# Feed-forward down projection: from eight block products per block pair to seven, on one Trainium2 core

## The reference, cut to what matters

```
x = x + merged @ w_o
h = _rms_norm(x, g_ffn)
u = jnp.square(jax.nn.relu(jnp.einsum('bld,df->blf', h, w_up)))    # D_MODEL = 2048 -> D_FF = 8192
return x + jnp.einsum('blf,fd->bld', u, w_down)                    # 8192 -> 2048
```

## Time and profile before

| | us |
|---|---|
| median of three runs | 3292.89 (3292.1 to 3293.08) |
| the profiled execution: span | 3293.0 |
| PE busy in it | 3158.8 (96%) |
| DVE busy | 1949.6 (59%) |
| ACT busy | 1439.7 (44%) |
| up projection, from its first loads to its last matmul | about 1885 to 2528 |
| down projection with the output | 2528 to 3293 |

### The profile page before, as it was taken

The page is one execution under the profiler, slowest core; times in us unless marked ns, Lnnn a source line. Parts: engine busy times, 40 slices in busy tenths (PEclk is TensorE's granted clock), DMA queues, the critical chain, the costliest instruction groups (busy, mean ns, idle before and its releaser), DMA issues.

```text
span 3293.0 us, 66551 instructions
## 1 busy us (share of the span) xinstructions
PE 3158.8 (96%) x24759; PEld 3020.4 (92%) x24759; DVE 1949.6 (59%) x2700; ACT 1439.7 (44%) x1998; POOL 342.2 (10%) x623
## 2 busy tenths in 40 slices
PE   6999999999999999899889699999999999999999
PEld 6999999999999998775389699999999999999999
DVE  4225666665555558899843687887876333433333
ACT  4224666665555556677722344444443122121211
POOL 1111111111111113233300000000000000000000
PEclk9999999999999999999999899999999999999999
DMA  6434333333343338799953244444445323333322
GB/s 186 114 107 110 102 97 99 106 101 93 108 114 93 106 96 297 270 362 326 377 188 102 90 129 128 128 132 135 135 134 191 128 93 115 115 117 122 120 90 91
DMA packets 506127, 472.92 MB, mean 144 GB/s; under 512 B 19680, under 2 KB 435312, under 8 KB 504856
## 3 DMA queue, kind: packets, MB, share of 16 engines
q1 hardware_dynamic: 465616, 353.80, 36.1%
q0 software_dynamic: 40416, 117.93, 10.4%
HBM read 426.85 MB, written 44.80 MB: 143 GB/s over the span
## 4 chain that ended last, share of the span: by engine, by line
PE 88%; DVE 6%; DMA 3%; ACT 1%; issue 1%; POOL 0%; SPq 0%; POOLq 0%; ACTq 0%; DVEq 0%
PE ps L901 26%; PE ps L902 26%; PE ps L903 26%; PE ps L1084 3%; PE ps L1095 2%; PE ps L1096 2%; PE ps L1017 2%; DMA pg<-in_cache_fox_v_dram 1%; DVE pg_lo L1773 1%; PE ps L1127 1%; PE ps L1126 1%; PE ps L948 1%; DMA x2T<-xT_dram 0%; DVE qp_lo L1773 0%; DVE w_lo L1773 0%
## 5 line engine op out<-in xcount | busy, mean ns | idle before, releaser
L901 PE MATMUL ps<-h_hi,w_hi 128*128 128x260 f32 (+1 forms) x2592 | 750.0, 289 | 16.1 <-DVE h_lo L1773 13.0
L902 PE MATMUL ps<-h_hi,w_lo 128*128 128x260 f32 (+1 forms) x2592 | 737.3, 284 | 0.0
L903 PE MATMUL ps<-h_lo,w_hi 128*128 128x260 f32 (+1 forms) x2592 | 736.5, 284 | 0.0
L1773 DVE TENSOR_TENSOR w_lo<-w_raw,w_hi 128x2048 fp32r<-128x2048 f32 (+1 forms) x241 | 466.8, 1937 | 275.4 <-ACT w_hi L1323 239.6
L1323 ACT ACTIVATE w_hi<-w_raw 128x2048 fp32r<-128x2048 f32 x160 | 305.9, 1912 | 693.0 <-PE ps L903 680.1
L901 PE MATMUL ps<-ub_hi,w_hi 128*128 128x260 f32 x2048 | 581.6, 284 | 9.9 <-DVE xd L2184 5.5
L903 PE MATMUL ps<-ub_lo,w_hi 128*128 128x260 f32 x2048 | 580.4, 283 | 0.0
L902 PE MATMUL ps<-ub_hi,w_lo 128*128 128x260 f32 x2048 | 580.2, 283 | 0.0
L901 PE MATMUL ps<-b_hi,w_hi 128*128 128x260 f32 x1792 | 508.3, 284 | 29.6 <-DVE b_lo L1773 25.2
L901 PEld LDWEIGHTS ps<-h_hi,w_hi 128*128 128x128 f32 x2592 | 491.4, 190 | 19.6 <-DVE h_lo L1773 14.5
L902 PE MATMUL ps<-b_hi,w_lo 128*128 128x260 f32 x1792 | 508.3, 284 | 0.0
(11 more groups left out here) (303 smaller groups left out, 5160.4 us busy)
## 6 DMA issues: line engine op xcount, KB each, us to landing
w_raw<-in_w_in_dram SPq DMA_DIRECT2D x81, 1024.0 KB, 5.7
w_raw<-in_w_down_dram SPq DMA_DIRECT2D x64, 1024.0 KB, 5.4
w_raw<-in_w_up_dram SPq DMA_DIRECT2D x32, 1024.0 KB, 8.3
x2T<-in_w_up_dram SPq DMA_DIRECT2D x64, 512.0 KB, 5.4
pg<-in_cache_sb_v_dram POOLq DMA_DIRECT2D x106, 256.0 KB, 4.9
w_raw<-in_cache_fox_k_dram SPq DMA_DIRECT2D x72, 256.0 KB, 5.4
u_dram<-x2T SPq DMA_DIRECT2D x64, 260.0 KB, 3.0
u_st<-u_dram SPq DMA_DIRECT2D x8, 2080.0 KB, 7.8
```

Of the source, the lines that this page charges most:

```text
L901: pe.matmul(out, whi, xhi, start=first, stop=False, skip_group_check=more)
L902: pe.matmul(out, wlo, xhi, start=False, stop=False, skip_group_check=more)
L903: return pe.matmul(out, whi, xlo, start=False, stop=last, skip_group_check=more)
L1773: return dve.tensor_tensor(out, a, hi.bitcast(F32), ALU.subtract)
```

## The change: what it does, and the diff

The down projection gets the form of the up projection. The 8192 hidden features are taken in 4 chunks of 2048 (two halves, even and odd blocks, of 8 blocks each); in a chunk there are 8 pairs of output blocks, and each pair is a 2x2 block product of seven products (`down`, the same `product`, `high`, `low` and `weight_sum` as in the up projection). There are 4 x 8 x 7 = 224 products of 24 matmuls.

The seven token operands of a chunk (u11, t6, u21, t5, u12, t7, t4: blocks of u and differences of them) are formed in the up projection: DVE gets four more subtractions of 128 x 260 for a pair (t5, t6, t7 in the place of u12, t4), and POOL stores seven such blocks a pair (`store`) where SP stored four. At the start of each chunk the seven operands for the whole chunk (128 x 2080 each, 1.065 MB) are loaded one after the other into `b_lo`'s slot (`block_load`), each as soon as the last pair of the chunk before has finished the product that used this slot. For slots 0, 2, 4 and 6 ACT then makes the high part and DVE the low part in place. For slots 1, 3 and 5 (`NEG`) ACT makes the high part and then writes its negative into the low part's place, and a transfer issued by POOL adds the operand from DRAM to it (`block_add`, two transfers of half the block each with `accum_op`). There is one set of slots, not two.

The results go straight from the accumulation banks to `xd` by seven additions of DVE, the first 780 wide, the others 260 wide. The weights are loaded in four quarters of 0.5 MB a pair, in both projections, from a single list (`weights`); one of the quarters (`a22`) has two buffers, the others have one, and each is reloaded as soon as the low part that read it last is made. Their runs in DRAM are 512 bytes long (1024 bytes before in the down projection). The order of loads, ACT and DVE in the up projection changes a little: low part 4 comes before the first weight sum, low part 5 comes after the second. The turned result goes back into `xd` in place of `yn`, for each pair two quarter-megabyte stores.

```diff
-S_WO, S_FF = 81, 97
-FC = 1024
-NC = FF // FC
+S_WO = 81
 NU = FF // (2 * P)
-KF = FC // P
+KF = 8
+NC = NU // KF
...
+NEG = (1, 3, 5)
...
-        u_dram = nc.dram_tensor("u_dram", [FF // P, P, TQ], F32).ap()
+        u_dram = nc.dram_tensor("u_dram", [7, P, NU, HQ], F32).ap()
...
+        b_raw = b_lo[:, :, :, :].bitcast(F32)
+        xd = at("xd", [P, KT, TQ], F32, at_r)
+        u7 = [x2T[:, 8:15, HQ * i:HQ * i + HQ] for i in range(2)]
+        u_p1, u_p16, u_p165 = (x2T[:, k, 0:HQ] for k in (7, 6, 5))
...
+        a11, a12, a21 = w_raw[0][:, 0:8, :], w_raw[0][:, 8:16, :], w_raw[1][:, 0:8, :]
+        a22 = [w_raw[1][:, 8:16, :], a22_odd[:, :, :]]
...
+            def weights(g, b11, b12, b21, b22):
+                wait(sp, a_lo, count(g, 7, -7))
+                sp.dma_start(a22[g.p], b22).then_inc(a22_ld[g.p], 16)
+                wait(sp, a_lo, count(g, 7, -5))
+                sp.dma_start(a11, b11).then_inc(a11_ld, 16)
+                wait(sp, a_lo, count(g, 7, -2))
+                sp.dma_start(a21, b21).then_inc(a21_ld, 16)
+                wait(sp, a_lo, count(g, 7, -1))
+                sp.dma_start(a12, b12).then_inc(a12_ld, 16)
...
+            def store(g):
+                pool.wait_ge(r_ok, count(g, 2, 2))
+                pool.wait_ge(u_ok, count(g, 3, 3))
+                pool.wait_ge(t_ok, count(g, 4, 4))
+                dst = u_dram[:, :, g.n:g.n + 1, :] if not g.mult else u_dram[:, :, bass.ds(g.x * 2 + g.n, 1), :]
+                pool.dma_start(dst.rearrange("s p o t -> p s (o t)"), u7[g.p]).then_inc(u_sv[g.p], 16)
...
+            def block_load(g, c, i):
+                pool.wait_ge(p_ok, count(g, 7, i + 1))
+                pool.dma_start(b_raw[:, i, :, :], u_dram[i, :, c * KF:c * KF + KF, :]).then_inc(blk_ld[i], 16)
+            def block_add(g, c, i):
+                pool.wait_ge(blk_neg, count(g, 3, NEG0 + NEG.index(i) + 1))
+                for k in (0, 4):
+                    pool.dma_start(b_raw[:, i, k:k + 4, :], u_dram[i, :, c * KF + k:c * KF + k + 4, :],
+                                   accum_op=ALU.add).then_inc(blk_ld[i], 16)
...
+            for i in range(7):
+                block_load(Pair(NU - 1), 0, i)
+                if i == 0:
+                    store(Pair(NU - 2))
+                if i == 4:
+                    block_add(Pair(0), 0, 1)
+            for i in (3, 5):
+                block_add(Pair(0), 0, i)
+            store(Pair(NU - 1))
+            pool.wait_ge(x2_sw, 16)
+            for p in range(2):
+                pool.wait_ge(u_sv[p], 8 * NU)
+            pool.dma_start(xd[:, 4:KT, :], x2_dram[:, 4:KT, :]).then_inc(xd_ld[1], 16)
...
+            for c in range(1, NC):
+                for i in range(7):
+                    block_load(Pair(NU + KF * c - 1), c, i)
+                    if i == 4:
+                        block_add(Pair(c), c, 1)
+                for i in (3, 5):
+                    block_add(Pair(c), c, i)
...
+                if fresh is not None:
+                    i = AT[o]
+                    if i in NEG:
+                        pe.wait_ge(blk_ld[i], count(fresh, 48, 64))
+                    else:
+                        pe.wait_ge(blk_lo, count(fresh, 4, i // 2 + BLK0 + 1))
...
-            def down(c, par, u, j, first=False, between=None):
...
-                                        k == 0, k == KF - 1)
-                        mm.then_inc(dense_ok, 1)
...
+            def down(g, fresh=None, turned=None):
+                a, b, c = g.p, 2 + g.p, 4 + g.p
+                if g.q == 1:
+                    pe.wait_ge(r_ok, 2 * NU)
+                    pe.wait_ge(c_ev, 5 * NU)
+                pe.wait_ge(e_ok, count(g, 7, -14 + 3))
+                product(g, 1, a, True, False, fresh)
+                pe.wait_ge(e_ok, count(g, 7, -14 + 6))
+                product(g, 6, b, True, False, fresh)
+                pe.wait_ge(e_ok, count(g, 7, 1))
+                product(g, 2, a, False, False, fresh)
+                if turned is not None:
+                    turn(turned)
+                pe.wait_ge(e_ok, count(g, 7, 2))
+                product(g, 5, b, False, False, fresh)
+                pe.wait_ge(e_ok, count(g, 7, -14 + 7))
+                product(g, 7, c, True, False, fresh)
+                if turned is not None:
+                    turn_samples(turned)
+                pe.wait_ge(e_ok, count(g, 7, 4))
+                product(g, 3, b, False, False, fresh)
+                pe.wait_ge(e_ok, count(g, 7, 5))
+                product(g, 4, c, False, False, fresh)
...
+            def block_high(c, i):
+                act.wait_ge(blk_ld[i], count(c, 48 if i in NEG else 16, 32))
+                act.activation(b_hi[:, i, :, :], b_raw[:, i, :, :], ACT.Copy).then_inc(blk_hi, 1)
+                if i in NEG:
+                    act.wait_ge(blk_hi, count(c, 7, i + BLK0 + 1))
+                    act.activation(b_lo[:, i, :, :], b_hi[:, i, :, :].bitcast(F32), ACT.Copy, scale=-1.0).then_inc(blk_neg, 1)
...
+            def down(g, nxt, old=None, new=None, done=None):
+                high(g, 7)
+                if old is not None:
+                    block_high(old, 4)
+                high(g, 3)
+                if old is not None:
+                    block_high(old, 5)
+                if new is not None:
+                    block_high(new, 0)
+                high(g, 4)
+                if old is not None:
+                    block_high(old, 6)
+                if new is not None:
+                    block_high(new, 1)
+                if done is not None:
+                    turned(done)
                 if nxt is not None:
+                    high(nxt, 5)
+                    high(nxt, 1)
+                if new is not None:
+                    block_high(new, 2)
+                if done is not None:
+                    turned_samples(done)
+                if nxt is not None:
+                    high(nxt, 6)
+                if new is not None:
+                    block_high(new, 3)
+                if nxt is not None:
+                    high(nxt, 2)
...
+            def block_low(c, i):
+                if i in NEG:
+                    return
+                dve.wait_ge(blk_hi, count(c, 7, i + BLK0 + 1))
+                minus(b_lo[:, i, :, :], b_raw[:, i, :, :], b_hi[:, i, :, :]).then_inc(blk_lo, 1)
...
+                low(g, 4)
+                weight_sum(nxt, 1)
                 dve.wait_ge(p_ok, count(g, 7, 4))
+                dve.tensor_tensor(u_p165, u_p1, b, ALU.add).then_inc(c_ev, 1)
+                if new is not None:
+                    block_low(new, 0)
+                weight_sum(nxt, 2)
+                low(nxt, 5)
                 dve.wait_ge(p_ok, count(g, 7, 5))
                 dve.wait_ge(c_ev, count(g, 5, 2))
+                wait(dve, u_sv[g.p], count2(g, 16, 0))
+                dve.tensor_tensor(u22, u_p165, c, ALU.add).then_inc(c_ev, 1)
+                low(nxt, 1)
+                relu_square(u22, 3)
+                if new is not None:
+                    block_low(new, 1)
+                weight_sum(nxt, 3)
+                dve.wait_ge(p_ok, count(g, 7, 6))
+                dve.tensor_tensor(u12, u_p1, b, ALU.add).then_inc(c_ev, 1)
+                low(nxt, 6)
+                relu_square(u12, 4)
+                dve.wait_ge(r_ok, count(g, 2, 2))
+                dve.wait_ge(u_ok, count(g, 3, 2))
+                dve.tensor_tensor(t5, u12, u11, ALU.subtract).then_inc(t_ok, 1)
+                if new is not None:
+                    block_low(new, 2)
+                dve.wait_ge(p_ok, count(g, 7, 7))
+                dve.tensor_tensor(u21, u_p16, c, ALU.add).then_inc(c_ev, 1)
+                dve.wait_ge(t_ok, count(g, 4, 1))
+                dve.tensor_tensor(t6, u22, t5, ALU.subtract).then_inc(t_ok, 1)
+                dve.tensor_tensor(u12, u22, u12, ALU.subtract).then_inc(t_ok, 1)
+                low(nxt, 2)
+                relu_square(u21, 5)
+                weight_sum(nxt, 4)
+                dve.wait_ge(u_ok, count(g, 3, 3))
+                dve.wait_ge(t_ok, count(g, 4, 2))
+                dve.tensor_tensor(t4, u21, t6, ALU.subtract).then_inc(t_ok, 1)
+                if new is not None:
+                    block_low(new, 3)
...
+            def down(g, nxt, old=None, new=None):
+                m = 2 * g.q
+                a, b, c = (ps[:, r + g.p, 0:HQ] for r in (0, 2, 4))
+                x11, x12, x21, x22 = (xd[:, m + i, h * HQ:(h + 1) * HQ] for i in range(2) for h in range(2))
+                x3 = xd[:, m:m + 2, :].rearrange("p m t -> p (m t)")[:, HQ:4 * HQ].rearrange("p (o t) -> p o t", o=3)
+                def add(n, x, bank, before=None):
+                    dve.wait_ge(p_ok, count(g, 7, n))
+                    if before is not None:
+                        dve.wait_ge(e_ok, count(g, 7, before))
+                    dve.tensor_tensor(x, x, bank, ALU.add).then_inc(e_ok, 1)
+                if g.q in (0, 2):
```

(47 more changed lines are left out.)

514 lines of the change are left out of this document (198 added, 316 removed).

## The result

The changed kernel takes 3341.48 us (median of 4 runs, 3337.87 to 3344.11) against 3292.98 for the kernel before: 1.5% slower, ratio 1.0146 with a 95% interval of 1.0131 to 1.016. The forecast was 3228, range 3194 to 3265: wrong in sign, and outside the range by 76 us. The profiled execution has a span of 3340.0 us.

A forecast was written before the change was run, and what follows sets the result against it. The prediction took PE's number of matmuls as the bound. A floor of 3184.7 us, + 31.6 for boundaries, + 2.2 store, + 4 clock, - 2.7 up projection's start, + 8 a21 loop, gave 3227.8; range 3194 to 3265.

The forecast's parts named there:

- The removed work: Down projection: 5376 matmuls in place of 6144, 768 fewer at 0.1197 us, 91.9 us saved.
- change-over wait of the old kind: Between up and down projection: 16.3 us of waits and slow clock, expected to go.
- half shared, the load takes about 4.9: Up projection: a21's load overlapping POOL's store takes 4.9 us, period 20.3 to 20.4, +8 us in all, ends 0 and 25.
- The loop: Up projection: a21's single-buffer load, first weight sum, DVE's work (15.4 us) and low part 7 follow one another each pair.
- the lone load: Up projection: a 512 KB quarter by itself lands in 3.9 us, for a period of 19.4 us, hidden.
- 31.6 + 2.2 + 4: Chunk boundaries: block transfers 7.9 us late at each of four, first boundary's store +2.2, slow clock after waits +4.
- slot 5 then follows in time: Chunk boundary: after lateness at slots 1 and 3, together 7.9 us, slot 5 adds none.
- runs beside the transfers' lateness: Chunk boundary: DVE's overrun, 1 to 2 us for each of two pairs, overlaps late transfers and adds nothing.
- the adding transfer: Chunk boundary: an add costs the same as a plain transfer of its size; upper end twice that, 5.1 us for 1.065 MB.
- The clock: Chunk boundaries: lower clock after PE's waits costs 1 us each, +4, from 0.8 us behind one earlier gap.
- The loop in full force: Rival, chance 0.18: a21's loop makes up pairs 20.9 us, 17 us over the forecast, 3245.
- The slower rival: Chance 0.06: adding transfers at boundaries are a slow kind; 9.0 us each to pass 3299.6, 3312 at 10 us.

The follow-up runs named there:

- run 2: The changed kernel with low part 7 of the next pair moved on DVE ahead of the fourth weight sum and the last subtraction: 3269.26 us, ratio 0.9926.
- run 6: The changed kernel with POOL's store of pair n held until the first weight sum for pair n + 2 is made: 3270.17 us, ratio 0.9935.
- run 8: run 2's kernel with DVE's additions 4 and 5 before the first weight sum ahead of a chunk, weights 2 ahead of blocks 3 and 2: 3256.48 us.
- run 7: run 2's kernel with PE's loop over the first three chunks of the down projection written out: 3256.9 us, ratio 0.9888.
- run 3: The changed kernel without the adding transfers, so its results are wrong (a probe of time alone): 3329.66 us.
- run 10: run 9's kernel without the adding transfers, the low parts in slots 1, 3 and 5 staying negative high parts: 3244.09 us.
- run 9: The changed kernel with the three edits of run 2, run 7 and run 8 together: 3260.71 us, ratio 0.9905.
- run 12: run 11's kernel with block loads 1 to 6 held back until a21 and a12 land, and DVE's block 3 low part moved later: 3269.07 us.
- run 11: run 9's kernel with DVE making all seven low parts, without negative copies or adding transfers: 3250.36 us, ratio 0.9868.

## Why the prediction was wrong

Point by point, by its own steps.

**The removed work was right.** 5376 matmuls, 20.1 us a down pair, and no change-over wait of the old kind. The sum of the parts reproduces the span within 1 us. (The start of the up projection was forecast 2.7 us shorter and came 6.0 shorter.)

**The up projection: right mechanism, wrong size, by 62 us.** The step that failed is "half shared, the load takes about 4.9". The loop was named with the right links and nearly the right length on DVE (15.4 predicted, 15.3 measured); the lone load was right (3.9 predicted, 3.9 measured in runs 2 and 6). The load beside the store took 7.35 us up to the sum in the pair shown and lands after 7.0 in the median. I had sized the collision as a fair share of two streams over their overlap, 1.0 us. It cost 3.1. And I had bounded the load from above by the 5.4 us of a group of four, a row in which a transfer competes only with its own queue; no row showed two queues meeting in full, so this was not a bound. A period of 15.4 plus a load L is a slope of 1 us a pair, 30 us in all, for each microsecond of L above 4.7: so sensitive a term should have carried a wide end of its own.

**The boundary: 92.5 us for a predicted 31.6 + 2.2 + 4.** The step that failed is its model: I asked when the blocks land, and took everything else as hidden beside it. PE's list above shows what was late at the second boundary: first DVE's fourth addition (2.56), because a weight quarter took 9.2 us to land and DVE keeps its order; then PE's own instructions after the jump (4.29 and 2.12); only then a block transfer (5.54), the third add. The runs give sizes to these, with the others in place: order on DVE 3 us a boundary in the mean (run 8), the jump 6 at each of the two boundaries that have one (run 7), the adds 3 to 4 (runs 3 and 10). They can't be summed, since behind each wait stands the next (run 9). Two sentences of the prediction were plainly wrong: "slot 5 then follows in time", and that DVE's and ACT's overrun "runs beside the transfers' lateness". The waits came one after the other, not side by side. And the adding transfer was mis-sized too: I took a plain one's cost, with twice that as the upper end. The two halves of the third add at the second boundary, issued when no block load was left ahead of them, landed after

```profile
b_lo<-u_dram POOLq DMA_DIRECT2D x2, 520.0 KB, 7.0
```

in the median (5.7 and 8.2; window 2802.9:2803), the whole 8.7 us after the first was issued, beside weight quarters. The first block of that chunk, as many bytes in one plain load, took 5.1, most of it before a quarter was issued beside it. In the prediction's terms, less 2.3 us for the way from issue to landing, that is an estimated 6.4 us for 2.5, over its upper end of 5.1.

**The clock was undersized.** I took 1 us a boundary. At the second boundary the waits of the list sum to 14.9 us, of 23.6 lost; the rest, 8.7 us, is matmuls started further apart. The clock was at its lower level (0.50) in three stretches that lie in or behind these waits, 20.4 us in all, with 3.9 us of the waits inside them; half of the other 16.5 is 8.3:

```profile
2772.20:2775.60 3.40, 2.98 (x14) 2.99 (x15) 3.40 (x3) 3.37 (x4) 0.82 (x2) 0.50 1.03 420
2785.80:2796.00 10.20, 8.08 (x38) 7.78 (x37) 5.04 (x5) 2.88 (x2) 0.73 (x1) 0.50 1.02 290
2809.70:2816.50 6.80, 5.47 (x25) 5.50 (x26) 3.64 (x4) 0.47 (x1) 0.00 (x0) 0.50 0.54 152
```

Over the four boundaries PE's waits sum to 60.8 of the 92.5 us; the other 31.7 are matmuls started further apart, where I had 4. A window of 10 us, nearly full of work, has 60 matmuls at clock 0.70, where 86 are in one at clock 1.00:

```profile
2790.00:2800.00 10.00, 9.87 (x60) 9.87 (x61) 6.30 (x6) 5.86 (x5) 0.00 (x0) 0.70 0.83 194
2820.00:2830.00 10.00, 10.00 (x86) 10.00 (x86) 7.28 (x8) 3.79 (x4) 0.00 (x0) 1.00 0.23 65
```

That one window cost 26 x 0.12 = 3.1 us, 0.1 of it a wait. My 0.8 us was from a single window of 5 us behind a single gap.

**The rivals.** The loop in full force was on the list, at 20.9 us a pair; it came at 22.4. The slower rival had the right sign for the wrong reason: adds of 9 us as the sole cause. Halves of an add did land 9.0 us after issue in the median, but many stood behind block loads; taking the adds away gave back 12 us (run 3), where this rival needed 103. What was missing was a case in which several middling losses come together, each with its own place. The chance of 0.06 for slower rested on one mechanism having to carry 103 us alone.

## What to carry to other kernels

A load with a single buffer, an engine that keeps its order, and the work in between make a loop: work out its period for the slowest landing that any other queue can cause, and expect each microsecond over PE's own period to be paid at every turn. A large transfer that is released at a stage's end should be held against everything else that must get through the DMA engines in those microseconds: small loads in short pieces on another queue, and, when a long loop jumps back, its instructions. Where an order is written out by hand, ask at each wait not only who needs this result but what stands behind it; in runs 9 and 12 one wait that was taken away only uncovered the next.

## What the hardware did that I had not expected

A 512 KB load in pieces of 512 bytes, 3.9 us by itself, took 7.0 us (median) beside one 910 KB store in pieces of 1040 bytes. Beside a row of 1 MB loads in pieces of 8320 a12 and a22 took 18 to 23 us without adds (run 11) and up to 29 with them. An add of 1.06 MB in two halves was complete 8.7 us after issue, where a plain load of it took 5.1. The jump back of a long PE loop came with waits of 4.3 us at its target and 2.1 us 16 matmuls further on, and with an instruction transfer landing in each; with the loop written out a boundary was 6 us shorter and the second wait was gone, and the profile had put the first one down to DVE. The kernel with one more wait that was always met already ran 27 us slower, and no run shows why.
